# The scans of the second block placed between the low halves of the weights, and the gated product on GpSimd

## What is computed

```python
u = h @ w_in[l]
rg_x, rg_z, ml_x, ml_o, ml_z = jnp.split(u, split_pts, axis=-1)
y_rg = rglru(causal_depthwise_conv(rg_x, ...), ...) * jax.nn.silu(rg_z)
y_ml = mlstm_branch(ml_x, ml_o, ...) * jax.nn.silu(ml_z)

def rglru(x, ...):
    a = jnp.exp(log_a)
    u = jnp.sqrt(-jnp.expm1(2.0 * log_a)) * (i * x)
    # h[t] = a[t] * h[t-1] + u[t], over 512 tokens
    ...
def mlstm_branch(xm, ...):
    xc = jax.nn.silu(causal_depthwise_conv(xm, conv_w, conv_b))
    q, k = block_diag(xc, w_q), block_diag(xc, w_k)
    ...
```

## Time and profile before

| | us |
|---|---|
| median of 3 runs | 2152.99 |
| lowest, highest | 2151.70, 2153.58 |
| the profiled execution | 2151.8 |
| its span (first to last instruction) | 2149.9 |

### The profile page before, as it was taken

How to read it: one execution, slowest core, us unless ns; L and a number is a source line. 1 busy time by engine, 2 the same in 40 slices (tenths; PEclk the granted TensorE clock), 3 DMA queues, 4 the chain that set the end, 5 groups by cost and what they waited for, 6 DMA issues and landing times.

```text
span 2149.9 us, 22200 instructions
## 1 busy us (share of the span) xinstructions
PE 2012.4 (94%) x8726; PEld 1539.1 (72%) x8726; DVE 1274.7 (59%) x1837; ACT 847.4 (39%) x1271; POOL 357.4 (17%) x319
## 2 busy tenths in 40 slices
PE   7999999988878799999999899799999897999997
PEld 5888888756534488888887678676788676866886
DVE  5763444668797346655655777824773559435842
ACT  5331333201445643312333438444542365444531
POOL 2000001155333010000011202401201013102002
PEclk9999999988789999999999899899999898999998
DMA  4232232221000135645642132221132222220221
GB/s 179 93 120 82 96 105 94 80 62 62 15 1 1 64 133 168 204 172 176 198 145 69 49 105 79 78 79 50 49 96 93 87 85 70 69 89 30 89 90 58
DMA packets 53175, 196.72 MB, mean 92 GB/s; under 512 B 5968, under 2 KB 6480, under 8 KB 52432
## 3 DMA queue, kind: packets, MB, share of 16 engines
q1 hardware_dynamic: 42912, 159.50, 21.9%
q0 software_dynamic: 7504, 28.58, 4.1%
q10 hardware_dynamic: 2656, 7.23, 1.0%
HBM read 192.14 MB, written 2.10 MB: 90 GB/s over the span
## 4 chain that ended last, share of the span: by engine, by line
PE 79%; DVE 13%; ACT 4%; POOL 1%; DMA 1%; issue 1%; SPq 0%; POOLq 0%; DVEq 0%; ACTq 0%
PE PS L531 78%; DVE AR L1712 2%; DVE AR L1484 2%; DVE AR L1938 2%; DVE WLO L1481 1%; ACT WHI L1021 1%; DVE AR L1808 1%; DVE HNL L1484 1%; PE PS L726 1%; DVE TMP L1484 1%; DVE ACC L1484 0%; DMA RAW<-in_w_in 0%; DMA RAW<-in_w13a 0%; DVE AR L1819 0%; DVE AR L1909 0%
## 5 line engine op out<-in xcount | busy, mean ns | idle before, releaser
L531 PE MATMUL PS<-HNH,WHI 128*128 128x512 f32 x1632 | 663.9, 407 | 19.8 <-ACT HNH L1052 14.2
L1481 DVE TENSOR_TENSOR WLO<-RAW,WHI 128x1024 fp32r<-128x1024 f32 (+1 forms) x270 | 371.5, 1378 | 504.6 <-ACT WHI L1021 504.4
L531 PE MATMUL PS<-HNH,WLO 128*128 128x512 f32 x1632 | 644.4, 395 | 21.6 <-DVE WLO L1481 21.6
L1021 ACT ACTIVATE WHI<-RAW 128x1024 fp32r<-128x1024 f32 (+1 forms) x270 | 296.0, 1097 | 730.4 <-PE PS L531 643.7
L531 PE MATMUL PS<-HNL,WHI 128*128 128x512 f32 x1632 | 438.0, 391 | 0.2
L531 PEld LDWEIGHTS PS<-HNH,WHI 128*128 128x128 f32 x1632 | 311.1, 191 | 104.4 <-issue 24.0
L531 PEld LDWEIGHTS PS<-HNH,WLO 128*128 128x128 f32 x1632 | 311.4, 191 | 96.0 <-DVE WLO L1481 23.0
L531 PEld LDWEIGHTS PS<-HNL,WHI 128*128 128x128 f32 x1632 | 307.7, 189 | 66.2 <-DVE HNL L1484 2.1
L531 PE MATMUL PS<-AR 128*128 128x512 f32 (+12 forms) x700 | 205.3, 505 | 11.2 <-DVE SQ L1701 3.8
L2058 POOL TENSOR_TENSOR ACC<-ACC,SQ 128x512 f32<-128x512 f32 x46 | 62.7, 1363 | 789.2 <-ACT SQ L1036 788.2
L531 PEld LDWEIGHTS PS<-AR 128*128 128x128 f32 (+5 forms) x700 | 95.4, 188 | 89.4 <-issue 58.5
(11 more groups left out here) (294 smaller groups left out, 2514.7 us busy)
## 6 DMA issues: line engine op xcount, KB each, us to landing
RAW<-in_w_in SPq DMA_DIRECT2D x80, 512.0 KB, 3.5
AR<-in_w_ada POOLq DMA_DIRECT2D x48, 512.0 KB, 3.9
RAW<-in_w13a SPq DMA_DIRECT2D x44, 512.0 KB, 3.3
RAW<-in_w13b SPq DMA_DIRECT2D x44, 512.0 KB, 4.2
RAW<-in_w_out SPq DMA_DIRECT2D x40, 512.0 KB, 3.5
RAW<-in_w2a SPq DMA_DIRECT2D x16, 704.0 KB, 4.1
RAW<-in_w2b SPq DMA_DIRECT2D x16, 704.0 KB, 5.5
RAW<-in_w_inA SPq DMA_DIRECT2D x12, 512.0 KB, 3.2
```

What stands on the lines that cost most here:

```text
L531: return pe.matmul(o, l, r, start=start, stop=stop, skip_group_check=True)
L1021: act.activation(hi_of(name, i), raw_of(name, i), ACT.Copy).then_inc(*HI.up(name, i))
L1481: dve.tensor_tensor(lo_of(name, i), raw_of(name, i), f32(hi_of(name, i)), S_).then_inc(*LO.up(name, i))
```

## The change

DVE no longer runs the eight scans in a row. Scan m stands in iteration m, behind LO(m+3); the product rg_z goes one iteration later, xlo two. The gated product rg_y goes to POOL, which interleaves its rg_in, xc and rg_y. ACT's program keeps its order and waits for rg_y on POOL's counter.

```diff
@@ ACT
-                            act.wait_ge(*V.at("rg_y", l, 7))
+                            act.wait_ge(*G.at("rg_y", l, 7))
...
-                    act.wait_ge(*V.at("rg_y", l, m))
+                    act.wait_ge(*G.at("rg_y", l, m))
@@ DVE
+                def rg_z(m):
+                    dve.wait_ge(*A.at("rg_z", l, m))
+                    dve.tensor_tensor(RX[:, m, :], RX[:, m, :], bank("w_in2", 40 * l + 8 + m)[:, :], M_).then_inc(*V.up("rg_z", l, m))
+
                 for m in range(8):
+                    lo_next()
                     dve.wait_ge(*G.at("rg_in", l, m))
                     dve.tensor_tensor_scan(out=CX[:, m, :], data0=RX[:, m, :], data1=IX[:, m, :], initial=0.0, op0=M_,
                                            op1=A_).then_inc(*V.up("rg_h", l, m))
...
-                for m in range(8):
-                    lo_next()
-                    dve.wait_ge(*A.at("rg_z", l, m))
-                    dve.tensor_tensor(RX[:, m, :], RX[:, m, :], bank("w_in2", 40 * l + 8 + m)[:, :], M_).then_inc(*V.up("rg_z", l, m))
-                    mine()
-                    dve.tensor_tensor(Y[:, m, :], Y[:, m, :], RX[:, m, :], M_).then_inc(*V.up("rg_y", l, m))
                     for c in CONV_AT.get(8 + m, ()):
                         conv_x(c)
                     if m:
-                        xlo(m - 1)
+                        rg_z(m - 1)
+                    if m > 1:
+                        xlo(m - 2)
+                rg_z(7)
                 for h in range(4):
                     if h == 0:
+                        xlo(6)
                         xlo(7)
@@ POOL
-                for m in range(8):
+                def rg_in(m):
...
+                def rg_y(m):
+                    pool.wait_ge(*V.at("rg_z", l, m))
+                    pool.tensor_tensor(Y[:, m, :], Y[:, m, :], RX[:, m, :], M_).then_inc(*G.up("rg_y", l, m))
+
+                for m in range(3):
+                    rg_in(m)
                 for m in range(8):
+                    if m + 3 < 8:
+                        rg_in(m + 3)
                     pool.wait_ge(*A.at("xc", l, m))
                     pool.tensor_tensor(XC[:, m, :], XC[:, m, :], IX[:, m, :], M_).then_inc(*G.up("xc", l, m))
+                    if m:
+                        rg_y(m - 1)
+                rg_y(7)
```

More of the change, by code:

```diff
@@ L1935, in dve_program, with xlo @@
                         conv_x(c)
+                def xlo(m):
+                    dve.wait_ge(*A.at("xhi", l, m))
+                    dve.tensor_tensor(XLO[m], XC[:, m, :], f32(XHI[m]), S_).then_inc(*V.up("xlo", l, m))
+                def rg_z(m):
+                    dve.wait_ge(*A.at("rg_z", l, m))
+                    dve.tensor_tensor(RX[:, m, :], RX[:, m, :], bank("w_in2", 40 * l + 8 + m)[:, :], M_).then_inc(*V.up("rg_z", l, m))
                 for m in range(8):
+                    lo_next()
                     dve.wait_ge(*G.at("rg_in", l, m))
@@ L1939, in dve_program @@
                                            op1=A_).then_inc(*V.up("rg_h", l, m))
-                def xlo(m):
-                    dve.wait_ge(*A.at("xhi", l, m))
-                    dve.tensor_tensor(XLO[m], XC[:, m, :], f32(XHI[m]), S_).then_inc(*V.up("xlo", l, m))
-                for m in range(8):
-                    lo_next()
-                    dve.wait_ge(*A.at("rg_z", l, m))
-                    dve.tensor_tensor(RX[:, m, :], RX[:, m, :], bank("w_in2", 40 * l + 8 + m)[:, :], M_).then_inc(*V.up("rg_z", l, m))
-                    mine()
-                    dve.tensor_tensor(Y[:, m, :], Y[:, m, :], RX[:, m, :], M_).then_inc(*V.up("rg_y", l, m))
                     for c in CONV_AT.get(8 + m, ()):
```

## The result

| | before | changed |
|---|---|---|
| median, us | 2152.99 (2151.70 to 2154.54) | 2161.91 (2157.89 to 2164.82) |
| runs | 5 | 5 |
| profiled span, us | 2149.9 | 2159.1 |

The change makes the kernel slower: ratio 1.0045, 95% interval 1.0029 to 1.0061, some 9 us. The forecast was 2174, 21 us. The sign and the closed loop held, the size was more than twice too large.

A forecast was written before the change was run, and what follows sets the result against it. The prediction took PE, busy 94% of the span, as the bound. Each of two layers gets 10.8 us longer, 21.6 together; 2151.8 + 21.6 = 2173.4, against the median 2174.6, so forecast 2174, range 2156 to 2182.

The forecast's parts named there:

- closed loop: Low half, scan, two sigmoids, high part, high half across DVE and ACT: 6.1 us an iteration, where PE needs 5.44.
- ordinary iteration: Iteration without convolution: POOL's gated product starts 0.1 us ahead of the low half, adding 1.2 us, 7.2 in all.
- the moved scans alone would break even: Scans between low halves, without POOL's gated products: old PE stall gone, scan 7 ends at 1390.1, no net change.
- The hold of the low half by the gated product: DVE's low half waits until POOL's gated product, ahead by 0.1 us, ends: 1.2 us in each ordinary iteration.
- The chain that makes the end late: After scan 7, sigmoids, POOL products, bank emptying and last halves start the eleventh query tile at 1413.8 instead of 1403.04.
- Rival (a): Low half starts before POOL's gated product; those iterations take 6.1 us, 6.3 more a layer, 2166 in all; chance 0.24.
- rival (b): Not slower: POOL's products fall into DVE's waits for ACT and hold nothing; 2150, or 2126 at best; chance 0.12.
- The step that failed: Scan length on DVE: taken as 2.24 us each, from eight in a row, with POOL only slowed beside them.
- The second term: Collision of a DVE instruction with two SBUF inputs and a POOL product: one waits for the other, 1.3 us each.
- rival (c): Scans wait for POOL products too, 1.3 us each, eight times: 10.4 us more a layer, 2195; chance 0.05.
- Rival (d): PE idles around query tiles, then runs at half clock: 2.6 us a stretch, up to 2179; counted within the forecast's 0.5.
- All there is to win: 26.8 us: PE's 10.8 us wait for a low half plus 2.6 us at half clock, 13.4 us in each of two layers.

The follow-up runs named there:

- e2: Changed kernel with the gated product back on DVE, scans still between the low halves: 2150.99 us, ratio 0.9987 to the kernel before.
- e4: Changed kernel with ACT making its high halves one tile further ahead, gated product still on POOL: 2151.05 us, ratio 0.9993 to the kernel before.
- e6: Changed kernel with POOL running the gated product of tile m-2 when scan m ends, ahead of xc(m): 2155.40 us, ratio 1.0011 to the kernel before.
- e1: Kernel before with every scan waiting for the last of POOL's eight rg_in products: 2161.4 us, a single run.
- e3: Kernel before with the gated product on POOL and the scans still in a row: 2150.84 us, ratio 0.9999 to the kernel before.
- e8: Kernel before with two low halves moved into the row of scans, after scans 1 and 5: 2143.13 us, ratio 0.9952.
- e7: Changed kernel with the gated product back on DVE and ACT's high halves one tile ahead: 2144.53 us, ratio 0.9960 to the kernel before.

## Why the prediction was right and wrong, by its steps

| step of the prediction, layer 0 | forecast | measured |
|---|---|---|
| closed loop without the gated product | 6.1 | 5.3 (e2) |
| ordinary iteration of the changed kernel | 7.2 | 7.1 with a POOL product beside the scan, 5.95 to 5.98 without |
| iterations with a convolution | 9.9 | 9.5 |
| end of scan 0 | 1346.6 | 1343.34 + 2.30 = 1345.6 |
| end of scan 7 | 1401.1 | 1393.19 + 2.30 = 1395.5 |
| emptying of the query banks begins | 1407.1 | 1398.74 + 2.30 = 1401.0 |
| eleventh query tile, first matmul | 1413.8 | 1404.36 + 2.30 = 1406.7; its first low half at 1405.53 + 2.30 = 1407.8 |
| longer by, a layer | 10.8 | 4.5 and 4.9 |

**What held.** The closed loop through ACT, with the gated product in it (34.6 us of ACT waiting for scans; e4 opens it and wins 5.7 us). That the moved scans alone would break even (e2). The hold of the low half by the gated product, by a margin of 0.17 us where 0.1 was forecast (e6 takes most of it away). The chain that makes the end late: scan 7, two sigmoids, three POOL products, eight emptied banks, the last halves. Its length from scan 7 to the first emptied bank was 5.5 us, forecast with 5.7 and hand-overs. Rival (a), the low half wins the race, did not happen; rival (b) did not either.

**The step that failed** is the scan. The prediction took 2.24 us as its own length and wrote of rows 5 and 7 "neither waited for the other, POOL was only slower". Both waited, in turn, which e1 shows: 1.2 us alone. In the sum that is 1.1 us too much for each of scans 5, 6 and 7, where POOL is silent: 3.3 of the 5.6 us by which scan 7 came early. It also made the closed loop by itself look slower than PE, 6.1 against 5.44, where e2 measures 5.3. The second term is the collision: taken as 1.2 to 1.3 us, near the length of POOL's row, it measures 1.06 to 1.09 for a whole one (3.39 - 2.33 for the convolution, 2.31 - 1.22 for a low half) and 0.94 to 0.98 for the low halves of the last iterations, where POOL was ahead by 0.17 us and more. By the ends of the scans this makes 0.4 us in each of the two iterations with a convolution and 0.1 to 0.2 in the last three, some 1.3 in all. The remaining 1.0 came before the first scan's end: its low half was forecast to be held for 1.2 us by rg_in(3) and took 1.30 in all, while the hold sat in the 2.24 us of the scan already.

The Trainium skill, page "SBUF — State Buffer", section "Who interferes with whom", has the rule that I set aside in rival (c): a DVE instruction with two SBUF inputs contends with a GpSimd instruction that reads SBUF. For the scan the rows of e1 agree, 12.12 us against 17.38. The prediction did not only reject it, it also priced it the wrong way, as 10.4 us a layer on top. If exclusion holds, the 2.24 us of the row already contain the waiting, and the scan by itself is shorter; the rule would have lowered the sum, not raised it. A row in the same trace could have told me: two 128x512 scans of other operations, with POOL idle, on the timeline of DVE before, take

```profile
1445.18 1.23 DVE L1965 TENSOR_TENSOR_SCAN AR<-AR 128x512 f32<-128x512 f32 x1
...
1447.17 1.22 DVE L1969 TENSOR_TENSOR_SCAN AR<-AR 128x512 f32<-128x512 f32 x1
```

**Rival (d), half clock,** happened and cost little. PE did run slowly in parts (0.87 and 0.85 above), but the eleventh tile waits for its halves anyway, and those came from ACT and DVE; e4, with 2.5 us more of busy time in one layer than in the other and the same stretch, says the same. It was right to leave it out of the sum. Where PE itself is the bound the clock does count: the two layers of e3, with equal gaps, differ by 1.4 us.

**"All there is to win: 26.8 us"** was right as a bound and misleading as an aim: no version here wins more than 4.4 us a layer. Even in e8 and e7 PE still has 6.2 to 6.5 us of gaps in the stretch, mostly waits for low halves and for banks that DVE gives back. That DVE and POOL between them have little slack here is an argument, not a test: what holds the last microseconds stays open.

## What to carry to other kernels

- When work is moved between the steps that feed a pipeline, write down the loop that the program order now closes (here scan, sigmoid, high half, low half) and compare its length with the pace of the engine it feeds: 5.3 us against 5.44 without the POOL product, 6.0 with it. Whatever is added inside such a loop is paid every time: the product cost 6.0 us a layer in the closed loop, 3.2 with the loop open (e4 against e7), and nothing that can be told where PE itself was the bound (e3).
- If two neighbours in a trace both take longer than elsewhere and their pitches are equal, they are probably taking turns. Look for the same instruction with the other engine idle before taking its length as its own.
- To take away one stall, move only what it waits for. Two low halves in each row of scans (e8) won as much as moving all the scans with both repairs (e7), and the full change lost 9 us.

## What the runs showed of the hardware

- A scan of 128x512 with two operands in SBUF takes 1.21 us alone and 2.2 to 2.3 beside a POOL product of that size; eight in a row took 17.38 us with POOL busy and 12.12 with three POOL products among them. POOL's product goes from 1.30 to 2.15 at the same time.
- A whole collision costs DVE 1.06 to 1.09 us for a POOL product whose row reads 1.30; where the 0.2 us between them go, no run shows. A DVE product with one input in PSUM (rg_z) kept its 0.65 to 0.68 in these stretches of all versions.
- The order is decided by who starts first, even by 0.17 us: where POOL led by that, DVE's low half took 2.20 instead of 1.22. In e2 DVE's low part of XC starts 0.01 us before POOL's xc (1378.77 and 1378.78) and keeps its 0.68, and POOL's product takes 1.82.
- Gaps that are spread out can hide a loss: 11.7 us of gaps on PE after against 10.8 before, and a stretch 4.5 us longer. PE's busy time at a lower clock fills the difference, 70.7 us against 67.1 for the same 281 matmuls.
